# Hidden rows turned by VectorE instead of TensorE in the feed-forward loop of a decoder trunk

## What is computed

```
def swiglu_ffn(h, w_up, w_down):
    gate, up = jnp.split(h @ w_up, 2, axis=-1)
    return (jax.nn.silu(gate) * up) @ w_down

for l in range(DEPTH):                       # DEPTH 2, D_FF 2816
    x = x + 0.5 * swiglu_ffn(rms_norm(x, norm_ffn1[l]), ffn1_up[l], ffn1_down[l])
    ...                                      # the mixer, with x + merged @ w_out[l]
    x = x + 0.5 * swiglu_ffn(rms_norm(x, norm_ffn2[l]), ffn2_up[l], ffn2_down[l])
return rms_norm(x, final_norm)
```

## Time and profile before

| what | value |
|---|---|
| median of 3 runs | 1084.0 us (1083.89 to 1087.99) |
| profiled execution | 1084.53 us |
| its span | 1082.8 us |
| TensorE (PE) busy | 1072.5 us |
| VectorE (DVE) busy | 906.6 us |
| ScalarE (ACT) busy | 649.3 us |
| GpSimd (POOL) busy | 78.5 us |
| DMA | 215.78 MB, mean 199 GB/s |

### The profile page before, as it was taken

How to read it: one execution, slowest core, us unless ns; L and a number is a source line. 1 busy time by engine, 2 the same in 40 slices (tenths; PEclk the granted TensorE clock), 3 DMA queues, 4 the chain that set the end, 5 groups by cost and what they waited for, 6 DMA issues and landing times.

```text
span 1082.8 us, 15616 instructions
## 1 busy us (share of the span) xinstructions
PE 1072.5 (99%) x5212; PEld 894.3 (83%) x5212; DVE 906.6 (84%) x1247; ACT 649.3 (60%) x881; POOL 78.5 (7%) x102
## 2 busy tenths in 40 slices
PE   9999999999999999999999999999999999999997
PEld 6887778988988888888888888888899888888886
DVE  6999988766897699999889999986679877999996
ACT  6655655656964565655665655645569446665664
POOL 0034410100200000000000000001002000000000
PEclk9999999999999999999999999999999999999999
DMA  9577695653555557666647668848445555666761
GB/s 297 182 249 234 186 313 189 233 169 124 165 172 180 189 171 236 192 221 222 206 149 227 191 217 279 264 140 277 147 133 167 193 171 161 213 204 209 232 193 75
DMA packets 175420, 215.78 MB, mean 199 GB/s; under 512 B 40536, under 2 KB 138912, under 8 KB 174864
## 3 DMA queue, kind: packets, MB, share of 16 engines
q1 hardware_dynamic: 172928, 205.55, 58.9%
q0 software_dynamic: 2144, 9.12, 2.5%
q10 hardware_dynamic: 304, 0.53, 0.1%
HBM read 209.79 MB, written 5.24 MB: 199 GB/s over the span
## 4 chain that ended last, share of the span: by engine, by line
PE 90%; ACT 3%; DVE 3%; DMA 2%; issue 2%; POOL 0%; SPq 0%; DVEq 0%; ACTq 0%; POOLq 0%
PE psum L1775 28%; PE psum L1777 28%; PE psum L1776 28%; PE psum L1793 2%; PE psum L1874 1%; DMA raw<-ffn_up_dram 1%; DVE w_lo L1131 1%; ACT w_hi L728 1%; ACT xs L930 1%; DMA scores<-hid_blocks 1%; PE psum L1866 1%; DVE xs L1131 0%; PE psum L2092 0%; PE psum L2227 0%; DVE small_T L1131 0%
## 5 line engine op out<-in xcount | busy, mean ns | idle before, releaser
L1131 DVE TENSOR_TENSOR w_lo<-raw,w_hi 128x512 fp32r<-128x512 f32 (+4 forms) x282 | 412.8, 1490 | 76.7 <-ACT w_hi L728 75.4
L1775 PE MATMUL psum<-w_hi,xT 128*128 128x512 f32 (+2 forms) x984 | 383.0, 389 | 0.0
L1777 PE MATMUL psum<-w_hi,xT 128*128 128x512 f32 (+2 forms) x984 | 379.3, 385 | 0.0
L1776 PE MATMUL psum<-w_lo,xT 128*128 128x512 f32 (+2 forms) x984 | 378.8, 385 | 0.0
L728 ACT ACTIVATE w_hi<-raw 128x2048 fp32r<-128x2048 f32 (+5 forms) x166 | 282.6, 1708 | 72.7 <-PE psum L1777 66.9
L1775 PEld LDWEIGHTS psum<-w_hi,xT 128*128 128x128 f32 x984 | 184.7, 188 | 39.5 <-DVE w_lo L1131 1.2
L1777 PEld LDWEIGHTS psum<-w_hi,xT 128*128 128x128 f32 x984 | 184.7, 188 | 37.0
L1776 PEld LDWEIGHTS psum<-w_lo,xT 128*128 128x128 f32 x984 | 184.9, 188 | 34.7 <-issue 0.2
L859 ACT ACTIVATE oT<-xs 128x1024 fp32r<-128x1024 f32 x72 | 76.5, 1062 | 86.0 <-DVE xs L1131 86.0
L818 ACT ACTIVATE scores<-psum,stat 128x256 f32<-128x256 f32 x88 | 40.9, 469 | 86.1 <-PE psum L1777 84.9
L1131 DVE TENSOR_TENSOR oT<-xs,oT 128x1024 fp32r<-128x1024 f32 x72 | 87.8, 1223 | 0.0
(11 more groups left out here) (238 smaller groups left out, 1406.2 us busy)
## 6 DMA issues: line engine op xcount, KB each, us to landing
raw<-ffn_up_dram SPq DMA_DIRECT2D x170, 512.0 KB, 4.9
raw<-ffn_down_dram SPq DMA_DIRECT2D x44, 1024.0 KB, 5.0
raw<-w_in_dram SPq DMA_DIRECT2D x20, 1024.0 KB, 5.2
raw<-w_attn_proj_dram SPq DMA_DIRECT2D x8, 1024.0 KB, 5.0
raw<-w_out_dram SPq DMA_DIRECT2D x8, 1024.0 KB, 5.0
raw<-w_uq_dram SPq DMA_DIRECT2D x8, 576.0 KB, 4.1
hid_blocks<-scores SPq DMA_DIRECT2D x32, 128.0 KB, 2.0
scores<-hid_blocks SPq DMA_DIRECT2D x128, 32.0 KB, 4.2
```

What stands on the lines that cost most here:

```text
L1131: return dve.tensor_tensor(dst, a, b, ALU.subtract)
L1775: nc.tensor.matmul(dst, a_hi, b_hi, start=first, stop=False)
L1776: nc.tensor.matmul(dst, a_hi, b_lo, start=False, stop=False)
L1777: return nc.tensor.matmul(dst, a_lo, b_hi, start=False, stop=last)
```

## The change

Row block 1 of the hidden values goes the way of row block 0: turned by VectorE, stored, fetched. Chunk 1 goes this way too, with both row blocks. TensorE's turns are left in chunks 0 and 10 alone. The scratch and its three semaphores exist once per row block. Further:

- On TensorE THIRD of a chunk (`third`) stands behind the first up products of the next chunk, not at the chunk's end. `plain_used` tells when SECOND is done; plainA of row 0 and plainB wait for it, plainA of row 1 and the sums' splits wait for THIRD (`sums_free`).
- The weight splits of slots 2 and 0 are done in halves by ScalarE (`half_split`) and VectorE (`up_halves`). VectorE's slot 0 and its second half of the weight sums stand at the start of the next body.
- On SP the fetch of row 1 stands between the two up loads of the next chunk, and the fetch of row 0 waits for sumA.
- On GpSimd the window table is loaded after five rotary steps, and layer 0's second bias broadcast goes out in the middle of the rotary steps.

```diff
@@ sync: loads, stores, fetches @@
+            def fetch_hidden(L, f, j, t):
+                sp.wait_ge(hid_stored[t].sem, hid_stored[t].upto(L, (f * SEVEN + j) * 16))
+                if t == 0:
+                    sp.wait_ge(sumA_lo.sem, sumA_lo.upto(L, f * SEVEN + j))
...
+                store_hidden(L, f, 1, 0)
+                fetch_hidden(L, f, 1, 0)
+                store_hidden(L, f, 1, 1)
                 with nc.sync.Fori(3, NCH) as j:
                     load_up(L, f, q0 + j - 1, 2, j, 0)
+                    fetch_hidden(L, f, j - 2, 1)
                     load_up(L, f, q0 + j, 0, j, 1)
-                    store_hidden(L, f, j - 1)
+                    store_hidden(L, f, j - 1, 0)
                     load_seven(L, f, q0 + j, j - 1)
-                    fetch_hidden(L, f, j - 1)
+                    fetch_hidden(L, f, j - 1, 0)
+                    store_hidden(L, f, j - 1, 1)
                 load_down(L, f, q0 + NCH - 1, 2, NCH - 1)
+                fetch_hidden(L, f, SEVEN, 1)
@@ gpsimd @@
-                pool.dma_start(window[:, :], c_window.bitcast(F32R)).then_inc(const_landed, 16)
...
+                pool.dma_start(window[:, :], c_window.bitcast(F32R)).then_inc(const_landed, 16)
                 for unit in (1024.0, 1.0):
+                    if unit == 1.0:
+                        broadcast(gates[:, 1, :], b_gate[0:1, :], bias_landed)
...
                 for t in range(TB):
+                    if L == 0 and t:
+                        continue
@@ scalar @@
+            def plainA(L, f, d, t):
+                if isinstance(d, int) and d == 0:
+                    act.wait_ge(hid_copied.sem, hid_copied.upto(L, f + 1))
+                else:
+                    if t == 0:
+                        act.wait_ge(plain_used.sem, plain_used.upto(L, f * SEVEN + d))
+                    else:
+                        sums_free(L, f, d)
+                    act.wait_ge(hid_moved[t].sem, hid_moved[t].upto(L, moved_count(f, d)))
...
                 with nc.scalar.Fori(2, NCH - 1) as j:
-                    plainA(L, f, j - 1)
+                    plainA(L, f, j - 1, 0)
                     plainB(L, f, j - 1)
+                    silu_rows(L, f, j, 0)
+                    sums_free(L, f, j - 1)
+                    sumB_half(L, f, j - 1, 0)
+                    sumB_half(L, f, j - 1, 1)
+                    plainA(L, f, j - 1, 1)
                     sumA(L, f, j - 1)
-                    silu_rows(L, f, j, 0)
-                    sumB(L, f, j - 1)
-                    split(L, q0 + j, 2, None, u2 + j + 1)
+                    half_split(L, f, q0 + j, 2, j, u2 + j + 1)
                     silu_rows(L, f, j, 1)
-                    split(L, q0 + j + 1, 0, None, u0 + j + 2)
-                    copy_hidden(L, f, j)
+                    half_split(L, f, q0 + j + 1, 0, j, u0 + j + 2)
@@ vector @@
-                hidden_product(L, f, 1)
+                hidden_rows(L, f, 1, 0)
+                turn_blocks(L, f, 1, 0)
+                hidden_rows(L, f, 1, 1)
+                turn_blocks(L, f, 1, 1)
                 sumB_half(L, f, 0, 1)
                 split(L, q0 + 1, 2)
-                split(L, q0 + 2, 0)
-                with nc.vector.Fori(2, NCH - 1) as j:
+
+                def body(j):
+                    up_halves(L, f, q0 + j, 0, None if isinstance(j, int) and j == 2 else j - 1)
+                    if not (isinstance(j, int) and j == 2):
+                        sumB_half(L, f, j - 2, 1)
+                    plainA(L, f, j - 1, 0)
+                    plainB(L, f, j - 1)
+                    addB_first(L, f, j - 1)
+                    hidden_rows(L, f, j, 0)
+                    turn_blocks(L, f, j, 0)
+                    addB_second(L, f, j - 1)
                     addA(L, f, j - 1)
-                    plainA(L, f, j - 1)
-                    plainB(L, f, j - 1)
+                    plainA(L, f, j - 1, 1)
                     sumA(L, f, j - 1)
-                    hidden_rows(L, f, j, 0)
-                    turn_blocks(L, f, j)
-                    addB(L, f, j - 1)
-                    sumB(L, f, j - 1)
-                    half_split(L, q0 + j, 2, 0)
+                    sumB_half(L, f, j - 1, 0)
+                    if isinstance(j, int) and j == SEVEN:
+                        sumB_half(L, f, j - 1, 1)
+                    up_halves(L, f, q0 + j, 2, j)
                     hidden_rows(L, f, j, 1)
-                    half_split(L, q0 + j, 2, 1)
-                    split(L, q0 + j + 1, 0)
+                    turn_blocks(L, f, j, 1)
@@ tensor @@
+                def third(d):
+                    wait(sumB_lo, L, (f * SEVEN + d) * 2 + 2)
+                    wait(plainA_lo, L, plain_count(f, d, 1))
+                    seven(d, THIRD).then_inc(w_used.sem, 1)
+
                 def chunk(j):
                     d = j - 1
-                    wait(hid_copied, L, f * (SEVEN + 1) + d + 1)
+                    wait(act_done, L, (f * NCH + j - 1) * TB + TB)
                     up_rows(L, f, j, 0)
-                    wait(plainA_lo, L, f * (SEVEN + 1) + d + 1)
+                    if not (isinstance(d, int) and d == 1):
+                        third(d - 1)
+                    wait(plainA_lo, L, plain_count(f, d, 0))
                     wait(plainB_lo, L, f * SEVEN + d + 1)
                     seven(d, FIRST)
                     wait(act_done, L, (f * NCH + j) * TB + 1)
                     up_rows(L, f, j, 1)
                     wait(sumA_lo, L, f * SEVEN + d + 1)
                     wait(sumB_lo, L, (f * SEVEN + d) * 2 + 1)
-                    seven(d, SECOND)
-                    turn_hidden(L, f, j)
-                    wait(w_lo_done, L, RING * (q0 + j) + 2)
-                    seven(d, THIRD).then_inc(w_used.sem, 1)
+                    seven(d, SECOND).then_inc(plain_used.sem, 1)
 
                 def last_chunk():
                     j = NCH - 1
-                    wait(hid_copied, L, (f + 1) * (SEVEN + 1))
+                    third(SEVEN - 1)
+                    wait(act_done, L, (f * NCH + j - 1) * TB + TB)
                     up_rows(L, f, j, 0)
```

More of the change, by code:

```diff
@@ L835, in plainA @@
-            def plainA(L, f, d):
-                if not (isinstance(d, int) and d == 0):
-                    act.wait_ge(w_used.sem, w_used.upto(L, RING * (f * FFN2_0 // RING + d) + 2))
-                    act.wait_ge(hid_moved.sem, hid_moved.upto(L, moved_count(f, d)))
-                act.wait_ge(hid_copied.sem, hid_copied.upto(L, f * (SEVEN + 1) + d + 1))
-                for t in range(TB):
-                    last = act.activation(tile_rows(small_T[:, 0, 0:N512], t), hid_rows[t], ACT.Copy)
-                last.then_inc(plainA_hi.sem, 1)
+                high(L, hid_tr, 2 * f + 2, small_T[:, 0, hid_cols(j)], psum[:, TR_BANK, :], hid_hi)
@@ L880, in ffn @@
                 sumB_half(L, f, 0, 0)
-                copy_hidden(L, f, 0)
-                plainA(L, f, 0)
+                copy_hidden(L, f)
+                plainA(L, f, 0, 0)
+                plainA(L, f, 0, 1)
                 sumA(L, f, 0)
@@ L1385, in addA @@
                 tile = lambda i: hid_rows[i % 2][:, i // 2] if i < S1 else hid_sum(i)
-                if not (isinstance(d, int) and d == 0):
-                    dve.wait_ge(hid_moved.sem, hid_moved.upto(L, moved_count(f, d)))
-                dve.wait_ge(hid_copied.sem, hid_copied.upto(L, f * (SEVEN + 1) + d + 1))
-                if not (isinstance(d, int) and d == 0):
+                if isinstance(d, int) and d == 0:
+                    dve.wait_ge(hid_copied.sem, hid_copied.upto(L, f + 1))
+                else:
+                    for t in range(TB):
+                        dve.wait_ge(hid_moved[t].sem, hid_moved[t].upto(L, moved_count(f, d)))
                     dve.wait_ge(sumA_lo.sem, sumA_lo.upto(L, f * SEVEN + d))
@@ L1498, in ffn @@
                 split(L, q0 + j, 1)
+                plainA(L, f, SEVEN, 1)
                 join_second(L, f)
@@ L1871, in turn_hidden @@
                 wait(act_done, L, (f * NCH + j) * TB + TB)
-                for t in range(TB) if isinstance(j, int) and not 2 <= j < NCH - 1 else (1,):
+                for t in range(TB):
                     for k in range(KCH):
@@ L1916, in up_rows @@
                 for a, (q, r) in enumerate(((q0 + j - 1, 2), (q0 + j, 0))):
-                    hi, lo = weights(L, q, r)
+                    hi, lo = (w_hi[:, r, :], w_lo[:, r, :]) if a and t == 0 else weights(L, q, r)
                     for k in range(4):
+                        if a and t == 0 and k == 0:
+                            wait(half_lo, L, f * SEVEN + j - 1)
+                        elif a and t == 0 and k == 2:
+                            weights(L, q, r)
                         cols = slice(k * N512, (k + 1) * N512)
@@ L2006, in ffn @@
                 second_chunk()
-                with nc.tensor.Fori(2, NCH - 2) as j:
+                chunk(2)
+                with nc.tensor.Fori(3, NCH - 2) as j:
```

129 lines of the change are left out of this document (76 added, 53 removed).

## The result

| what | before | after |
|---|---|---|
| median of 6 runs each, same chip | 1085.13 us | 1093.44 us (1092.15 to 1094.28) |
| profiled execution | 1084.53 us | 1093.32 us |
| its span | 1082.8 us | 1091.6 us |

The change makes the kernel slower: ratio 1.0077, 95% interval 1.0065 to 1.0088. The forecast was 1083.5 us, no change, with a range that ended at 1093. The times of kernels are medians; of the kernel before with the extra turn, further down, two of eight executions took 1804 and 3840 us and are left out.

A forecast was written before the change was run, and what follows sets the result against it. TensorE, busy 99% of the span, was taken to bound the kernel, with VectorE 92% full in the loop. From 1084.5 us: +1.8 for four parts, -2.3 for the loads, 0.5 less for the median: 1083.5 us, range 1071 to 1093.

The forecast's parts named there:

- TensorE's floor: Feed-forward loop: without the pair of transposes (0.26 us), a chunk on TensorE takes 15.70 us instead of 15.96.
- VectorE's cycle: Feed-forward loop: 15.13 us of VectorE work plus 0.69 lost waiting, taken as 15.80 us a chunk, holds TensorE.
- The sum of a part: Each feed-forward part: six chunks -1.0, chunk 9 +1.1, entry +0.35, so +0.45 us; 1.8 us for four.
- The entry: Chunks 1 and 2 of each part: chunk 2 begins 0.8 us later, chunk 3 0.35 us later.
- The loads: First feed-forward part: moving the window table and a bias broadcast saves the 1.99 us stop and 0.3 more, 2.3 us.
- DMA and the queues: SP queue in the loop: row 1's blocks land by 6.5 to 8.5 us, before VectorE wants them at 9.0.
- the third rival: Loop: row 1 lands too late, 0.5 us in each of 28 chunks, + 14, giving 1098 us; chance 0.16.
- The gap's term: Loop: VectorE's waits before plainA's second row and the sums hold TensorE above its floor, 24 x 0.1 us.
- Moving third ... at no cost besides, but nothing waited there before: TensorE: putting THIRD behind the next chunk's first products works as described, costs nothing, and covers no earlier wait.
- The rival that the change could win: Whole kernel: VectorE keeps up everywhere, with gap and entry hidden, giving 1071.4 us; chance 0.12.

The follow-up runs named there:

- the kernel before with the extra turn: The kernel before, with VectorE also turning row 1 into a buffer nobody reads, TensorE's turn kept: 1088.2 us.
- the two other edits: The kernel after with layer 1's broadcasts moved to layer 0's mixer and chunk 1 turned by TensorE again: 1081.5 us.
- the version with all three edits: The kernel after with layer 1's broadcasts in layer 0's mixer, VectorE's first sums half before plainA row 1, chunk 1 turned by TensorE: 1071.53 us.
- E and S: The kernel after with layer 1's broadcasts in layer 0's mixer and VectorE's first half of the weight sums ahead of plainA row 1: 1078.9 us.
- kernel with S: The kernel after with VectorE's first half of the weight sums' split put ahead of plainA of row 1: 1084.69 us.

## Why the prediction was wrong, point by point

- **TensorE's floor, 15.70 us a chunk.** Right in kind, 0.06 high: 15.64 in the versions that reach it.
- **VectorE's cycle, 15.80 us, with its gap.** Right: 15.77 in part 3 (15.83 in part 2), with 0.37 us idle ahead of plainA's second row. The 0.2 forecast ahead of the sums is there too, too short for a bracket: 646.94 to 647.46 is 0.52 us where 0.34 was priced. The Trainium skill ("VectorE: DVE Perf Modes", section "The DRAIN you can't avoid") has the next instruction wait for an empty pipe, by which the cycle would be 16.9; the same section lets an instruction that is not held start earlier, which the prediction left out. With that exception the rows agree: starts lie some 0.08 us ahead of ends.
- **The sum of a part, +0.45 us.** Part 2, where nothing comes late, took 0.05 us more. Chunk 3 began 0.25 us earlier than before (0.35 later forecast), the next six chunks took 0.8 less (1.0 forecast), chunk 9 1.2 more (1.1 forecast). In part 1 the six chunks took as long as before and not 1.0 less: the prediction reckoned with chunks of 15.96 there, where they took 16.2 on average.
- **The entry.** Chunk 2 began 0.75 us later (0.8 forecast), in each part. In part 3 chunk 1's blocks reached ScalarE at 575.4 (576.2 forecast) and VectorE lost 1.05 us by them (1.4 forecast). What the step missed is that the blocks can come later still, as in part 4, and that TensorE's clock falls behind such a stop.
- **The loads.** 2.3 forecast. The stop near 158 is gone, as forecast, and taking the spread back costs the kernel after 2.6 us. But the stretch of part 1 became only 0.4 us shorter, where 2.3 less 0.45 was forecast.
- **The step that failed** is "DMA and the queues", its last sentence: "It holds, by 0.5 us at the worst of these." The landing times from which it took the worst (2.0 and 4.2 us) are the page's medians. With a 1 MB broadcast in flight the fetch took 6.9 us from the end of its issue. The broadcasts of layer 1 were in the trace of before, in the stretch that got the new wait, but the change does not touch them and nothing waited there, so I never set them beside the fetch. The price was in that trace as well, at the stop that the prediction did read: 6.7 us for the fetch behind the pair of part 1 (VectorE at 153.47). This is the third rival's mechanism, in three chunks of 28, and at 1.8 to 3.1 us each instead of 0.5. Part 3's stretch gives +6.2 of the +8.8 us where +0.45 was forecast; part 4's entry gives +2.9, part 1 -0.4 where -1.85 was forecast.
- **Slack was priced at nothing.** The gap's term was 24 x 0.1 us. Taking the gap away was worth 8.7 us in the kernel after and 10.0 on top of the two other edits: some 7 of it is pace and entry, the rest late arrivals that a VectorE busy 15.16 of 15.80 us can't take back.
- **"Moving third ... at no cost besides, but nothing waited there before"** was wrong. Nothing waited there before, but with VectorE carrying two turns something would: 6.7 us, shown in the version with all three edits, not in the kernel after.
- **The rival that the change could win** was underpriced: 1071.4 us was met to 0.1 us as soon as the three obstacles were out of the way, and small edits move them. (Chunk 1's transposes are back in that version, four times 0.5 us; the floor, 0.06 us lower in 24 chunks, makes up for 1.4 of it; the match to 0.1 us is luck.)

**Open.** Why the second store of chunk 1 takes 3.8 us to land in part 4 (2.0 in parts 2 and 3), and the blocks 2.4 us more than in part 2, isn't settled. It comes again in part 4, and in no other, in the kernels in which chunk 1 goes through the scratch: TensorE's stop there is 1.39 us with E and S (928.56). What else moves in that stretch was not taken apart. Also open is why most chunks with the gap take 15.87 us in parts 2 and 4 and 15.77 in part 3.

## What to carry to other kernels

When a change makes an engine wait for a transfer for the first time, lay every transfer of the whole program beside that wait, those of other queues and those that the change leaves alone too, and price the landing by the busiest stretch that the trace of before shows, not by the median. An engine at 96% of the cycle has little room to take a late arrival back, so look in its order for a wait that a swap of two instructions removes. And when one change bundles a gain with several small losses, take the losses out one by one before giving it up: here +0.8% became -1.25%.

## What I had not expected of the hardware

- How much a broadcast of GpSimd that goes out beside them delays SP's small transfers: 128 KB in four pieces took 6.9 us from the end of their issue, at 328 GB/s in all and a DMA share of 0.97.
- TensorE's clock did not fall behind stops of 1.99 and 2.20 us (703.21, kernel after), but did behind stops of 2.17 (940.99, kernel after), 2.33 (696.48, kernel with S) and 2.58 us (158.69, kernel before with the extra turn). Length alone doesn't tell; what else does is open. Some eight products then stood 0.43 us apart, about 1.6 us lost.
- VectorE's instructions are longer while GpSimd computes. In the version with all three edits, VectorE and GpSimd near 100 us:

```profile
100.30 1.30 DVE L1191 TENSOR_TENSOR oT<-xs,oT 128x1024 fp32r<-128x1024 f32 x1
101.53 0.51 DVE L1191 TENSOR_TENSOR small_T<-scores,small_T 128x256 fp32r<-128x256 f32 x1
```
```profile
100.62 1.39 POOL L628 TENSOR_SCALAR gates<-gates 128x128 f32<-128x128 f32 x1
```

The same two take 1.22 and 0.42 us at 109.43 and 110.56, when GpSimd is idle. The Trainium skill ("GPSIMD Engine Reference", section "1. Specifications") says that the two engines share their SBUF interfaces, with contention when a VectorE instruction has two SBUF inputs, as here; the rows agree, with 0.08 to 0.09 us for each instruction.
